# A two-layer encoder trunk in which row tile 0 is normed ahead of row tile 1, with eight places for split weights

## The reference, cut to what matters

```python
for l in range(DEPTH):                      # DEPTH = 2
    u = x @ w_in[l]                         # 2048 -> 12 column tiles of 512 (layer 1: 8 columns more)
    ...                                     # branches, concatenated: cat, 256 x 2048
    mix = cat @ w_out[l]
    x = layer_norm(ALPHA * x + mix, ln_mix_g[l], ln_mix_b[l])
    h = jnp.square(jax.nn.relu(x @ mlp_w1[l])) @ mlp_w2[l]   # 2048 -> 8192 -> 2048
    x = layer_norm(ALPHA * x + h, ln_mlp_g[l], ln_mlp_b[l])
return x
```

## Time and profile before

| | us |
|---|---|
| median of 3 runs | 2315.59 (2314.75 to 2318.05) |
| span of the profiled execution, first to last instruction | 2314.1 |
| TensorE busy | 2251.9 (97%) |
| VectorE busy | 1367.9 (59%) |
| ScalarE busy | 1068.1 (46%) |
| weights and other data read | 414.79 MB, 180 GB/s over the span |
| mean granted TensorE clock | 0.988 of full |

### The profile page before, as it was taken

One profiled execution on the slowest core, in us unless ns is written; L12 is line 12 of the kernel. 1 busy time (PEld: TensorE's weight loads), 2 busy tenths in 40 slices (PEclk: granted clock), 3 DMA queues, 4 the chain that ended last, 5 costly groups with the idle time before them and its releaser, 6 DMA issues.

```text
span 2314.1 us, 28894 instructions
## 1 busy us (share of the span) xinstructions
PE 2251.9 (97%) x10331; PEld 1868.4 (81%) x10331; DVE 1367.9 (59%) x1489; ACT 1068.1 (46%) x1163; POOL 34.1 (1%) x64
## 2 busy tenths in 40 slices
PE   8999999799999999999989999998999999999997
PEld 7888788688888888888878888887888888888885
DVE  4898986745545545545565545567455455455455
ACT  4555564354344344344344444434444444443543
POOL 2000000100000000000000000000000000000000
PEclk9999999899999999999999999999999999999998
DMA  7555545665665665666645555565656666656653
GB/s 240 170 158 158 170 127 177 190 197 189 192 189 185 191 190 183 197 184 189 193 156 162 166 180 164 168 192 177 188 189 194 184 190 193 184 189 194 188 188 122
DMA packets 213546, 418.70 MB, mean 181 GB/s; under 512 B 12777, under 2 KB 13857, under 8 KB 212400
## 3 DMA queue, kind: packets, MB, share of 16 engines
q1 hardware_dynamic: 211616, 406.90, 57.5%
q0 software_dynamic: 1808, 10.04, 1.2%
HBM read 414.79 MB, written 2.10 MB: 180 GB/s over the span
## 4 chain that ended last, share of the span: by engine, by line
PE 61%; issue 32%; DVE 5%; ACT 1%; DMA 1%; POOL 0%; POOLq 0%; SPq 0%; DVEq 0%; ACTq 0%
PE gemm L1210 19%; PE gemm L1212 19%; PE gemm L1211 19%; DVE lnp L969 1%; DVE w_lo L744 1%; PE pair L1330 1%; DMA raw<-in_ev_w_out 1%; DVE X L817 1%; DVE X L816 1%; PE pair L1563 1%; PE pair L1273 1%; ACT w_hi L440 0%; PE pair L1287 0%; PE pair L1403 0%; PE pair L1475 0%
## 5 line engine op out<-in xcount | busy, mean ns | idle before, releaser
L1084 DVE TENSOR_TENSOR w_lo<-raw,w_hi 128x1024 fp32r<-128x1024 f32 x508 | 621.6, 1224 | 663.2 <-ACT w_hi L647 663.2
L647 ACT ACTIVATE w_hi<-raw 128x1024 fp32r<-128x1024 f32 x508 | 537.8, 1060 | 774.5 <-PE gemm L1212 774.5
L1210 PE MATMUL gemm<-w_hi,x_hi 128*128 128x512 f32 x1792 | 710.5, 397 | 5.5 <-DVE w_lo L744 4.0
L1212 PE MATMUL gemm<-w_hi,x_lo 128*128 128x512 f32 x1792 | 702.2, 392 | 0.0
L1211 PE MATMUL gemm<-w_lo,x_hi 128*128 128x512 f32 x1792 | 701.7, 392 | 0.0
L1210 PE MATMUL gemm<-w_hi,c_hi 128*128 128x512 f32 x1280 | 500.8, 391 | 4.2 <-DVE X L772 2.5
L1212 PE MATMUL gemm<-w_hi,c_lo 128*128 128x512 f32 x1280 | 498.7, 390 | 0.0
L1211 PE MATMUL gemm<-w_lo,c_hi 128*128 128x512 f32 x1280 | 498.6, 389 | 0.0
L744 DVE TENSOR_TENSOR w_lo<-raw,w_hi 128x1024 fp32r<-128x1024 f32 x260 | 316.4, 1222 | 208.9 <-ACT w_hi L440 208.6
L440 ACT ACTIVATE w_hi<-raw 128x1024 fp32r<-128x1024 f32 x260 | 272.7, 1056 | 304.2 <-PE gemm L1212 276.8
L1210 PEld LDWEIGHTS gemm<-w_hi,x_hi 128*128 128x128 f32 x1792 | 339.2, 189 | 78.5 <-DVE w_lo L744 5.0
(11 more groups left out here) (195 smaller groups left out, 831.1 us busy)
## 6 DMA issues: line engine op xcount, KB each, us to landing
raw<-in_mlp_w SPq DMA_DIRECT2D x512, 512.0 KB, 3.9
raw<-in_ev_w_in SPq DMA_DIRECT2D x96, 512.0 KB, 3.7
raw<-in_od_w_in SPq DMA_DIRECT2D x96, 512.0 KB, 3.7
raw<-in_ev_w_out SPq DMA_DIRECT2D x32, 512.0 KB, 4.4
raw<-in_od_w_out SPq DMA_DIRECT2D x32, 512.0 KB, 4.4
lnp<-in_ln_mix_g POOLq DMA_DIRECT2D x2, 1024.0 KB, 5.9
lnp<-in_ln_mix_b POOLq DMA_DIRECT2D x2, 1024.0 KB, 9.2
lnp<-in_ln_mlp_g POOLq DMA_DIRECT2D x2, 1024.0 KB, 4.9
```

The source lines that it names most:

```text
L647: act.activation(w_hi[:, s % RING], raw[:, s % RING], ACT.Copy).then_inc(hi_ready, 1)
L1084: dve.tensor_tensor(w_lo[:, s % RING], raw[:, s % RING], w_hi[:, s % RING].bitcast(F32), ALU.subtract).then_inc(lo_ready, 1)
L1210: pe.matmul(acc[:, r, :], hi[:, k + c, rows], w_hi[:, slot, c, :], start=begin, stop=False)
L1212: ins = pe.matmul(acc[:, r, :], lo[:, k + c, rows], w_hi[:, slot, c, :], start=False, stop=end)
```

## The change

Four things change together.

1. **Row order in front of a norm.** In the MLP each tile is done in two halves of four chunks, and in each half row tile 0 passes its four chunks before row tile 1 does. In the last part of an output projection tiles 2 and 3 are taken together: row tile 0 of both, then row tile 1 of both. Both accumulators are acquired ahead of that. `chunk_used` is raised when row tile 1 has passed a chunk.
2. **Eight places** for `w_hi` and `w_lo` in the MLPs and in the first tile of layer 1 (`DEEP`, `slot_of`); the second four lie in scratch space that is free then. The `raw` ring keeps four.
3. **The norm per row tile**, in two passes on DVE alone: `centre` computes (x - mean)*gain, `scale` then times rstd plus offset. POOL takes one root per row tile. ACT norms nothing any more.
4. **Ten pieces** (`ORDER`) instead of five, one row tile each; TensorE transposes them in front of or halfway through chunks of the next tile (`tile_behind_norm`), or, for the first, halfway through the last chunk before the norm. At the end of the program there are six stores instead of five.

```diff
+DEEP = 2 * RING
+ORDER = [(0, 0), (0, 1), (0, 2), (1, 0), (1, 1), (1, 2), (0, 3), (0, 4), (1, 3), (1, 4)]
+STORES = [(0, 0, 8), (0, 8, 8), (1, 0, 4), (1, 4, 4), (1, 8, 4), (1, 12, 4)]
+def slot_of(s):
+    return (s + RING) % DEEP if deep(s) else s % RING
...
             def inverse_root(which):
-                pool.wait_ge(var_ready, 2 + which)
-                pool.tensor_tensor(rstd[:, :, 0], mv[:, :, 1], mhalf[:, 0:RT], ALU.pow).then_inc(rstd_ready, 1)
+                for r in range(RT):
+                    pool.wait_ge(var_ready, 2 + RT * (which - 1) + r + 1)
+                    pool.tensor_tensor(rstd[:, r, :], mv[:, r, 1:2], mhalf[:, 0:1], ALU.pow).then_inc(rstd_ready, 1)
...
+            def centre(r, k0, n_):
+                cols = slice(k0 * P, (k0 + n_) * P)
+                return mark(dve.scalar_tensor_tensor(out=X[:, r, cols], in0=X[:, r, cols], scalar=mv[:, r, 0:1],
+                                                     in1=lnp[:, 0, cols], op0=ALU.subtract, op1=ALU.mult))
+
+            def scale(r, k0, n_, centred):
+                cols = slice(k0 * P, (k0 + n_) * P)
+                dve.wait_ge(dve_link, centred)
+                dve.scalar_tensor_tensor(out=X[:, r, cols], in0=X[:, r, cols], scalar=rstd[:, r, :],
+                                         in1=lnp[:, 1, cols], op0=ALU.mult, op1=ALU.add).then_inc(normed, 1)
...
+            def layer_norm(which, s0, first_rows, second_rows, taken):
+
+                first_rows()
                 dve.wait_ge(lnp_loaded, 32 * which)
...
+                statistics(which, 0, taken)
+                c = [centre(0, *PIECES[i]) for i in range(3)]
+                rstd_wait(which, 0)
+                for i in range(3):
+                    scale(0, *PIECES[i], c[i])
+                row_lo(which, 0)
+                second_rows[0]()
+                row_lo(which, 1)
+                second_rows[1]()
+                statistics(which, 1, RT * NT)
+                row_lo(which, 2)
+                c = [centre(1, *PIECES[i]) for i in range(3)]
+                rstd_wait(which, 1)
+                scale(1, *PIECES[0], c[0])
+                scale(1, *PIECES[1], c[1])
+                row_lo(which, 3)
+                scale(1, *PIECES[2], c[2])
+                row_lo(which, 4)
+                upto(s0 + 4)
+                row_lo(which, 5)
+                scale(0, *PIECES[3], centre(0, *PIECES[3]))
+                upto(s0 + 5)
+                row_lo(which, 6)
...
+            def last_norm(first_rows, second_rows, taken):
+                first_rows()
+                dve.wait_ge(lnp_loaded, 32 * 4)
+                statistics(4, 0, taken)
+                c = [centre(*piece) for piece in STORES[:2]]
...
+            def mix_norm(layer):
                 upto(SLOT_MLP[layer] + RING - 1)
                 x_sums[0] += PARTS * NT
...
+                def first_rows():
+                    add_row(layer, PARTS - 1, NT - 2, 0)
+                    add_row(layer, PARTS - 1, NT - 1, 0)
...
+            IN_FRONT = {(0, 0): [1], (0, 1): [2], (1, 0): [4], (1, 1): [5], (1, 3): [6], (0, 7): [8]}
+            HALFWAY = {(0, 3): 3, (0, 5): 7, (1, 4): 9}
...
+                accs = [acquire(layer, t + j - TILE0[layer]) for j in range(2)]
+                for r in range(RT):
+                    for j in range(2):
+                        for i, k in enumerate(part[::CK]):
+                            if r == 0:
+                                pe.wait_ge(lo_ready, s + n_ * j + i + 1)
+                            final = r == RT - 1 and j == 1 and i == n_ - 1
+                            chunk_rows(accs[j], C_, r, k, s + n_ * j + i, i == 0, i == n_ - 1,
+                                       halfway=(lambda: row_piece(2 * layer + 1, 0)) if final else None)
...
+                    for half in range(CPT // RING):
+                        for r in range(RT):
+                            for c in range(RING * half, RING * (half + 1)):
```

486 lines of the change are left out of this document (268 added, 218 removed).

## The result

The changed kernel takes 2321.71 us (median of 19 runs, 2319.57 to 2324.91), the kernel before 2315.06 us (19 runs, 2312.03 to 2319.00). The ratio is 1.0026, 95% interval 1.0020 to 1.0032: slower by 0.3%, where 0.7% faster was forecast. The profiled execution has a span of 2320.0 us instead of 2314.1 (both as the page rounds them, to 0.1).

The account below looks back on a forecast made before the run. TensorE's matmuls were taken as the floor, so only its stalls at the four norm rows could move; gains 7.4+1.0+2.0+5.5 = 15.9 us took the median from 2315.6 to 2299.7 us, range 2290 to 2307.

Parts of the forecast that it names:

- The MLPs and the rest: nothing: Over 64 MLP tiles, eight places and row-wise halves change nothing; unrolled last block well under 1 us; bounds -1 to +2.
- The slower rival: In MLP half tiles, splits don't keep ahead of the row-wise order: 0.25 late in each of 128, 2331.7 us; chance 0.06.
- Norm row 2, -7.4: Behind the first MLP: the 6.42 us wait for the first normed piece goes, loss 4.5 instead of 11.9, 7.4 us gained.
- lead lost at row 2: Rival: at norm row 2 DVE is still busy with splits, so 7.4 becomes 1; total 2306.1 us; chance 0.05.
- clock falls: Rival: clock falls in norm row 3's wait, centring holds up roots, norm row 1 gains nothing; 2305.2 us; chance 0.15.
- Norm row 3, -2.0: Behind the second output projection: TensorE waits 1.85 for the accumulator and 2.9 for the first piece, yet 2.0 us gained.
- Norm row 1, -1.0: Behind the first output projection: TensorE waits 9.0 us early for the x_sum, DVE sets the time, 1.0 us gained.
- The end, -5.5: Norm row 4, at the program's end: last DVE operation ends sooner, span ends at 2308.6 instead of 2314.1, 5.5 us gained.
- the root: GpSimd's root beside DVE's centring at norm row 2: held up by the one running step, 0.48 us, costing nothing.

Follow-up runs that it names:

- e16: The changed kernel with the added weight places 192 bytes further on and, in each MLP's first block, the square ahead of ScalarE's last four splits: 2293.11 us.
- e1: The changed kernel, but in each MLP's first block ScalarE does tile 0's relu and square behind four of its eight weight splits: 2304.53 us.
- e2: e1 with the old chunk order inside the MLP, except the first tile behind a norm and the last ahead of one; eight places kept: 2305.57 us.
- e7: e1 plus 64 unused bytes before the scratch region; at norm rows 1 and 3 TensorE awaits the second accumulator only ahead of its own matmuls: 2316.93 us.
- e15: The changed kernel with only its added weight places moved 192 bytes further on, ScalarE's order as it was: 2311.28 us.
- e8: e7 with VectorE's first-row adds in front of norm rows 1 and 3 moved ahead of weight split base+3: 2309.46 us.
- e10: e1 with the edits of e7 and e8, without the 64 unused bytes, and the added weight places 1,216 bytes further on: 2291.15 us.

## Why the prediction was wrong

Forecast: 15.9 us gained in the profiled span. Measured: 5.9 lost. The difference of 21.8 is 16.9 in the two second tiles, 7.2 in the rest of the MLPs, less 2.2 by which the other parts came out better in sum (all from the unrounded rows).

- **"The MLPs and the rest: nothing"** is the step that failed, with its bounds of -1 to +2, twice.
  - It costed when a place comes free and when a chunk is split and loaded, and found slack in each. It didn't ask what is queued behind a split on the splitting engine. Before the change the eight splits of an up tile on ScalarE were for four chunks of this tile and four of the next, so the relu behind them waited for nothing that this tile's own end didn't bring. With eight places all eight run ahead of the next tile, while the raw ring of four lets only four be loaded. Behind a norm nothing has been loaded ahead, and the square waits 11 us. The prediction held both facts ("the raw ring stays at four", and the order of the loads) and used them only for VectorE's chain at the projections. Applied here, with the first four splits at 1601.2: 2.3 for both halves of a split and 3.9 for a load bring the fifth raw chunk at 1607.4, the eighth three splits of 1.2 later at 1611.0, its split ends at 1612.1, relu and square at 1614.2. TensorE wants the square 24 matmuls behind 1605.3, at 1610.7: 3.5 us late. It became 6 because the fifth chunk's load, issued at 1603.8, let ScalarE go on only at 1609.6, 5.7 later, and the next three followed 1.4 apart. Loads are slower in this kernel: the median of `raw<-in_mlp_w` is 4.8 us, where the earlier trace rows has 3.9.
  - The slower rival (splits that don't keep ahead, decided by 0.12 us a half tile) had the right sign and the wrong mechanism: TensorE waited for one low part in the first tile of each MLP, 0.51 us, and for none behind that. Splits did keep ahead; the work queued behind them did not.
  - The places were taken as alike. That a matmul's time depends on where its weights lie against its activations was in no row of the trace of before, since all places there have the same distance modulo 256; so it could not be costed from it, but it could have stood in the range: new operand addresses are something that the rows don't show. It cost 9.7 us in the MLPs beside those two tiles (e16 against e1: 4.67 and 4.99).
  - It also undersized a gain: 2.5 us (-1.50 and -0.98 in e16), which is why only 7.2 showed of the 9.7. In the kernel before they stand at four places, where TensorE's loop over the blocks turns, twice in each MLP; the profile shows nothing that is waited for there (`805.42 0.49 PE L1210 MATMUL gemm<-w_hi,x_hi 128*128 128x512 f32 x1 [0.47 <-issue]`). The change writes out the last block, so two of the four turns are gone, which the prediction put at well under 1 us; they cost 1.2 in that execution. The two that are left took 1.4 before and 0.2 in e16. That this is the deeper ring's doing is not shown: e2 has eight places as well and loses 0.8 us at one of them.
- **Norm row 2, -7.4:** right. -7.85 with the last MLP tile ahead of it, and no wait in front of the first piece, no low clock. The rivals "lead lost at row 2" and "clock falls" didn't come in there. The tile behind it starts at 1198.93 and not near 1191.8, since the first MLP had by then lost 11 us and norm row 1 had gained 3.9.
- **Norm row 3, -2.0:** right in its steps: the accumulator's wait 1.72 (1.85 forecast), the first piece's 2.80 (2.9). That the second tile starts at 1605.28 (1605.1 forecast) is in part luck: the losses and gains ahead of layer 1's second tile cancel to 0.2 us, and the row itself gave 1.6. That DVE's chain sets this row is shown by e7. The clock fell behind the 2.8 us (a mean of 0.65 from 1574 to 1577), as one rival had it. In e1, after a wait of 2.75, it stayed at 1.00, and the same row of the table is 405.4 us instead of 406.35: the fall cost about 0.9.
- **Norm row 1, -1.0:** the mechanism was right: the wait stood where it was forecast, at 6.58 instead of 9.0, and the first piece, for which TensorE waits 0.77, came at 437.1 instead of 439.0. In that execution the raw chunks landed sooner. It gave -3.9 instead of -1.0, but whether the size was off can't be told from one execution each: against the same trace of before, the nine kernels without an edit at that row gave from -5.1 (e16) to +0.3 (e15).
- **The end, -5.5:** right, -5.27, though the root took longer beside VectorE's work than taken. GpSimd's two roots of norm row 3 and the two at the end are

```profile
1571.93 0.73 POOL L381 TENSOR_TENSOR rstd<-mv,mhalf 128x1 f32<-128x1 f32 x1 [377.00 <-DVE mv L830]
1578.67 0.55 POOL L381 TENSOR_TENSOR rstd<-mv,mhalf 128x1 f32<-128x1 f32 x1 [6.01 <-DVE mv L830]
...
2305.19 1.52 POOL L381 TENSOR_TENSOR rstd<-mv,mhalf 128x1 f32<-128x1 f32 x1 [703.92 <-DVE mv L830]
2311.83 0.99 POOL L381 TENSOR_TENSOR rstd<-mv,mhalf 128x1 f32<-128x1 f32 x1 [5.12 <-DVE mv L830]
```

The second ran with VectorE idle: 0.55 is what this root takes by itself (the 0.72 of the earlier trace rows are of one for both row tiles). The others began while VectorE's first centring step ran, which took 0.47, 1.27 and 0.74 us, with the next step behind it without a gap. Each root ended about 0.4 us after the first step did (0.42, 0.42, 0.41), before the train was over. So the root was held by the one step that it met, as the prediction took it, and a long step held it longer. The Trainium skill (SBUF — State Buffer, Who interferes with whom) says that of two such instructions one blocks the other fully; the rows agree for the step that was running, and show no second blocking by the steps behind it. In the norm rows inside the program and at the end it cost nothing, since the scaling began behind the train.

Had the two faults not been in the kernel, the forecast of 2299.7 would have been 6.6 us above the 2293.1 of e16: 2.5 in the MLPs, and 4.1 at norm row 1, where that is inside the scatter.

**What stays open.** Norm row 1 differs from execution to execution more than anywhere else. From the first big matmul to the MLP's second tile the nine kernels without an edit there took from 457.3 (e16) to 462.7 us (e15), with 458.5 in the changed kernel and 458.2 in e1. The last raw chunks of the first output projection land late (in the changed kernel ScalarE stands 5.63 us for one and 2.56 for the next), and TensorE's wait for the accumulator there was 5.5 us in e16, 6.58 in the changed kernel and 11.5 in e15. So no difference under 5 us at that row is settled by one profile, and how much of e8's gain there is the edit's was not settled. Why the distance modulo 256 costs time, and why the excess runs on into well placed chunks, is not shown; only that it does. All operands here have float32 size and places that are whole multiples of 256 bytes long; other shapes were not run.

## What to carry to other kernels

When a buffer is made deeper, look on every engine at what is queued *behind* the instruction that now may run ahead, and whether each of the rings that feed it got deeper too: a split that waits for a load holds up work that needs neither. Run a change of places apart from a change of order. And compare the pitch of steady matmuls to the nanosecond, stretch by stretch, before any wait: 2 to 5 ns each over 3,072 matmuls on the added places, and what runs on behind them, is 10 us that no view of waits shows.

With both repairs and the edits of e7 and e8 (e10) the kernel takes 2291.15 us, 24 us below the kernel before in the same runs (2315.06) and 31 below the changed one. Its lead of 2 us over e16 is not clear of the spread of four runs each.
